# Choosing the experts' tokens in two halves: top-k on 48 partitions, a merge by a reversed list, and the first expert's rests on VectorE

## What is computed

```python
def _expert_choice(h, router_w, w1, w3, w2):
    ...
    C = max(1, EC_CAPACITY * N // N_EXPERTS)
    aff = jax.nn.softmax((xs @ router_w).astype(jnp.float32), axis=-1)
    gate, idx = lax.top_k(aff.T, C)
    xe = xs[idx]
    he = jax.nn.silu(jnp.einsum('ecd,edf->ecf', xe, w1)) * jnp.einsum('ecd,edf->ecf', xe, w3)
    ye = jnp.einsum('ecf,efd->ecd', he, w2) * gate[..., None].astype(h.dtype)
    out = jnp.zeros_like(xs).at[idx.reshape(-1)].add(ye.reshape(-1, D))
```

## Time and profile before

| | |
|---|---|
| median of 3 runs | 2005.06 us (2003.74 to 2011.64) |
| profiled execution: time, span | 2010.78 us, 2008.9 us |
| mean granted TensorE clock | 0.963 of 2.4 GHz |
| busy share TensorE, VectorE, ScalarE, GpSimd | 92%, 77%, 58%, 16% |
| mean DMA rate | 270 GB/s |

### The profile page before, as it was taken

One profiled execution on the slowest core, in us unless ns is written; L12 is line 12 of the kernel. 1 busy time (PEld: TensorE's weight loads), 2 busy tenths in 40 slices (PEclk: granted clock), 3 DMA queues, 4 the chain that ended last, 5 costly groups with the idle time before them and its releaser, 6 DMA issues.

```text
span 2008.9 us, 27163 instructions
## 1 busy us (share of the span) xinstructions
PE 1846.0 (92%) x9522; PEld 1304.3 (65%) x9522; DVE 1544.8 (77%) x2270; ACT 1156.3 (58%) x1540; POOL 326.2 (16%) x152
## 2 busy tenths in 40 slices
PE   4999999949999999999969999995999999999993
PEld 2776777836666666666657786784566666666662
DVE  4543646579999999999846364667899999999993
ACT  2410256337787877777642114623677777777772
POOL 0100021030212222121012003112122122122210
PEclk9999999969999999999989999996999999999997
DMA  9468201278999999999852721025799999999973
GB/s 342 163 226 321 84 1 31 107 289 332 368 385 379 376 378 383 386 386 377 289 188 87 261 80 79 9 108 231 296 378 370 386 374 386 376 388 380 383 299 128
DMA packets 86219, 542.02 MB, mean 270 GB/s; under 512 B 6880, under 2 KB 9698, under 8 KB 61572
## 3 DMA queue, kind: packets, MB, share of 16 engines
q1 hardware_dynamic: 75556, 504.10, 64.6%
q0 software_dynamic: 10592, 36.97, 6.8%
HBM read 517.19 MB, written 23.86 MB: 269 GB/s over the span
## 4 chain that ended last, share of the span: by engine, by line
PE 87%; DVE 7%; DMA 2%; ACT 2%; issue 1%; POOL 1%; SPq 0%; DVEq 0%; ACTq 0%
PE bank L1098 53%; PE bank L799 10%; PE bank L976 5%; PE bank L692 2%; PE bank L924 2%; PE bank L1115 1%; PE bank L835 1%; PE bank L939 1%; PE bank L909 1%; PE bank L1108 1%; PE bank L1014 1%; PE bank L997 1%; PE bank L1047 1%; DMA x_res<-arena_z,iscat 1%; DVE ring_r L1957 1%
## 5 line engine op out<-in xcount | busy, mean ns | idle before, releaser
L1378 ACT ACTIVATE arena_h_r<-ring 128x1024 fp32r<-128x1024 f32 x480 | 504.6, 1061 | 163.1 <-PE bank L1098 159.7
L1896 DVE TENSOR_TENSOR ring_r<-ring,arena_h_r 128x1024 fp32r<-128x1024 f32 x470 | 557.6, 1218 | 32.4 <-ACT arena_h_r L1378 25.3
L1098 PE MATMUL bank<-arena_h_r,arena_u_r 128*80 128x512 f32 x1280 | 372.8, 398 | 4.6 <-DVE arena_u_r L1916 4.6
L1896 DVE TENSOR_TENSOR ring_r<-ring,arena_u_r 128x1024 fp32r<-128x1024 f32 x282 | 333.8, 1219 | 13.7 <-ACT arena_u_r L1378 7.1
L1378 ACT ACTIVATE arena_u_r<-ring 128x1024 fp32r<-128x1024 f32 x288 | 301.2, 1059 | 61.0 <-PE bank L1098 61.0
L1098 PE MATMUL bank<-ring_r,arena_u_r 128*80 128x512 f32 x1024 | 318.4, 392 | 0.0
L1098 PEld LDWEIGHTS bank<-arena_h_r,arena_u_r 128*80 128x80 f32 x1280 | 188.2, 151 | 101.2 <-DVE arena_u_r L1916 6.2
L1098 PE MATMUL bank<-arena_u_r 128*80 128x512 f32 x768 | 216.9, 391 | 0.0
L1098 PEld LDWEIGHTS bank<-ring_r,arena_u_r 128*80 128x80 f32 x1024 | 151.9, 148 | 84.8 <-issue 0.7
L644 POOL DMA_INDIRECT x_res<-arena_z,iscat x32 | 91.6, 2861 | 643.3 <-DVE arena_z L1942 643.3
L1098 PE MATMUL bank<-arena_h_r,arena_z_r 128*80 128x512 f32 x640 | 181.2, 397 | 3.6 <-DVE arena_z_r L1931 3.6
(11 more groups left out here) (255 smaller groups left out, 2668.5 us busy)
## 6 DMA issues: line engine op xcount, KB each, us to landing
ring<-in_exp_w SPq DMA_DIRECT2D x192, 2048.0 KB, 10.1
ring<-in_ada_w SPq DMA_DIRECT2D x24, 2048.0 KB, 9.0
ring<-in_w_in SPq DMA_DIRECT2D x8, 2048.0 KB, 19.8
ring<-in_w_out SPq DMA_DIRECT2D x2, 4096.0 KB, 13.4
x_res<-arena_z POOLq DMA_DIRECT2D x10, 512.0 KB, 3.8
xn_dram<-arena_u POOLq DMA_DIRECT2D x10, 512.0 KB, 3.0
arena_z<-x_res SPq DMA_DIRECT2D x10, 512.0 KB, 6.1
arena_z<-x_res POOLq DMA_DIRECT2D x5, 512.0 KB, 3.6
```

Source lines behind the costliest of these rows:

```text
L1098: mm = pe.matmul(bank[out + n][0:CAP, :], xs[:, c, :], w[:, n * 512:(n + 1) * 512], start=(c == 0 and part == 0), stop=(c == KC - 1 and pa ...
L1378: act.activation(high[c], slot[s][:, c, :], ACT.Copy).then_inc(high_ready, 1)
L1896: v.tensor_tensor(slot_r[s][:, c, :], slot[s][:, c, :], high[c], ALU.subtract).then_inc(low_ready, 1)
```

## The change

The latents' affinities are transposed into two halves: latents 0 to 255 on partitions 0 to 15, latents 256 to 511 on partitions 32 to 47. One operation over 48 partitions and 256 columns then serves both, and each half yields its 64 best in descending order. The merge takes, for place i, the larger of the upper half's value i and the lower half's value 63 - i; that is exactly the set of the 64 best of both. For it the lists are turned to [64, 16] and the lower one is reversed by a matmul with a reversed unit matrix (`turn64`, a new 64x64 input loaded behind `w_out`). The context's list keeps its own two rounds, behind the merge, and its own trip through TensorE.

```diff
--- the top-k on VectorE
-                affinity_T(1, 0, LAT, bank[7][0:EXPERTS, :])
+                v.wait_ge(affT_mm, l * 2 + 1)
+                for at in (0, 32):
+                    ins = v.tensor_copy(affL[0][at:at + EXPERTS, :], bank[7][at:at + EXPERTS, 0:LHALF])
+                link(ins)
                 for turn in range(CAP_L // 8):
-                    top_round(turn, 0, LAT, 0, CAP_L)
+                    top_round(turn, affL, slice(0, TWO), 0, CAP_L)
...
-                    if turn == 4:
+                    if turn == 5:
                         h2(4)
-                    if turn == 5:
-                        logit_max(4, 5, bank[0][:, 0:EXPERTS])
-                    if turn == 6:
-                        affinity(2, 4, 5)
-                affinity_T(2, LAT, TOK, bank[5][0:EXPERTS, 0:P])
+                lists_cast()
+                logit_max(4, 5, bank[0][:, 0:EXPERTS])
+                lists_turned()
+                affinity(2, 4, 5)
+                lists_merged()
+                v.wait_ge(affT_mm, l * 2 + 2)
+                link(v.tensor_copy(affC[0], bank[5][0:EXPERTS, 0:P]))
--- the merge: upper = [64, 16] indices and values, turned_f and turned_v the reversed lower list
+                    v.tensor_tensor(first, g, turned_v, ALU.is_ge)
+                    v.tensor_tensor(gateT[0:CAP_L, :], g, turned_v, ALU.max)
+                    link(v.tensor_tensor(step, f, turned_f, ALU.subtract))
+                    link(v.tensor_tensor(step, step, first, ALU.mult))
+                    v.tensor_tensor(idxT[0:CAP_L, 0:EXPERTS], step, turned_f, ALU.add)
--- TensorE's order
                     w_out_half(n, 0)
+                    if n == 3:
+                        norm2_T(2)
+                        router(1)
                     w_out_half(n, 1)
...
-                w_out_half(4, 0)
+                router(2)
+                w_out_half(4, 0, 0, 6)
                 norm2_T(3)
-                router(2)
+                w_out_half(4, 0, 6, KC)
                 router(3)
-                w_out_half(4, 1, 0, KC // 2)
+                w_out_half(4, 1, 0, 3)
...
-                w_out_half(4, 1, KC // 2, KC)
+                w_out_half(4, 1, 3, KC)
+                pe.wait_ge(x1_done, l * NT + 4)
+                keep_clock(7, 1)
                 norm2_T(4)
-                pe.wait_ge(x1_done, l * NT + 4)
+                keep_clock(1, 1)
                 router(4)
--- the first matrix's rests on VectorE (GpSimd's first_rest and its calls are gone)
+                for c in range(4):
+                    first_rest(c)
                 rows(0, 0)
                 rows_rest(0, 0)
+                for c in range(4, KC):
+                    first_rest(c)
                 rest(w3_at(0), 1)
```

More of the change, by code:

```diff
@@ L188, in hybrid_prefix_diffusion_step @@
         g2e, s2e, xt = (sflat[:, a:a + KC * CAP].rearrange("p (c t) -> p c t", c=KC) for a in (640, 1280, 1920))
-        affT = [sflat[0:EXPERTS, a:a + TOK] for a in (0, 640)]
+        TWO = 32 + EXPERTS
+        LHALF = LAT // 2
+        affL = [sflat[0:TWO, a:a + LHALF] for a in (0, 256)]
+        affC = [sflat[0:EXPERTS, a:a + CTX] for a in (512, 1920)]
+        turn64 = sflat[0:CAP_L, 2048:2112]
+        upper, lower, picked = (sflat[0:CAP_L, a:a + 2 * EXPERTS] for a in (2112, 2144, 2176))
         gate1 = sb("gate1", [P, 2, D])
@@ L1064, in _ @@
                 router(3)
-                w_out_half(4, 1, 0, KC // 2)
+                w_out_half(4, 1, 0, 3)
                 pe.wait_ge(aff_done, l * 2 + 1)
                 for t in range(4):
-                    mm = pe.transpose(bank[7][0:EXPERTS, t * P:(t + 1) * P], aff[:, t, :], ident)
+                    at = t // 2 * 32
+                    mm = pe.matmul(bank[7][at:at + EXPERTS, (t % 2) * P:(t % 2 + 1) * P], aff[:, t, :], ident,
+                                   start=True, stop=True)
@@ L1074, in _ @@
+                for n, x in enumerate((topf, topv)):
+                    mm = pe.transpose(bank[1][0:CAP_L, n * EXPERTS:(n + 1) * EXPERTS], x[32:TWO, 0:CAP_L],
+                                      ident[32:TWO, 32:TWO])
+                mm.then_inc(top_mm, 1)
                 pe.wait_ge(aff_done, l * 2 + 2)
                 pe.transpose(bank[5][0:EXPERTS, 0:P], aff[:, 4, :], ident).then_inc(affT_mm, 1)
-                hold(pe, top_done, l + 1, const_in)
-                pe.transpose(bank[6][0:CAP, 0:EXPERTS], topf[:, :], ident[0:EXPERTS, 0:EXPERTS])
@@ L1079, in _ @@
-                pe.transpose(bank[6][0:CAP, EXPERTS:2 * EXPERTS], topv[:, :], ident[0:EXPERTS, 0:EXPERTS])\
-                    .then_inc(top_mm, 1)
+                pe.wait_ge(turn_in, l * 16 + 16)
+                pe.wait_ge(top_done, l * 3 + 2)
+                pe.matmul(bank[1][0:CAP_L, 2 * EXPERTS:4 * EXPERTS], turn64, lower, start=True, stop=True).then_inc(top_mm, 1)
+                pe.wait_ge(top_done, l * 3 + 3)
+                for n, x in enumerate((topf, topv)):
+                    mm = pe.matmul(bank[4][CAP_L:CAP, n * EXPERTS:(n + 1) * EXPERTS], x[0:EXPERTS, CAP_L:CAP],
+                                   ident[0:EXPERTS, 0:EXPERTS], start=True, stop=True)
@@ L1884, in _ @@
                 v.tensor_copy(icur[1][:, :], idxT[:, 1:2]).then_inc(icur_done, 1)
[L1885 to L1890, removed]
+                v.tensor_copy(gateT[CAP_L:CAP, :], bank[4][CAP_L:CAP, EXPERTS:2 * EXPERTS]).then_inc(top_out, 1)
                 def rest(m, s, after={}):
```

77 lines of the change are left out of this document (44 added, 33 removed).

## The result

The changed kernel took 2023.7 us (median of 6 runs, 2018.45 to 2026.03), the kernel before, run beside it, 2007.9 us (2003.74 to 2012.41). The ratio is 1.0085, 95% interval 1.0064 to 1.0105: slower by about 16 us, outside the forecast range of 1991 to 2016 us. The profiled execution took 2020.89 us with a span of 2019.1. One execution of a later kernel, e3, took 3130.72 us at a granted clock of 0.557 and stands outside its ratio.

A forecast was written before the change was run, and what follows sets the result against it. TensorE, busy 92% of the span, was taken as the bound, with VectorE 7% of the chain of waits. Per layer +7.4 - 9.7 + 3.3 - 1.0 = 0.0, so 2005 us, range 1991 to 2016 us.

The forecast's parts named there:

- What bounds the kernel: TensorE 87% of the chain, VectorE 7%, the latter between last output projection and first expert product, where the change works.
- Term 2: From the top-k's opening copy to the second icur column: 32.9 us becomes 23.2, -9.7 us per layer.
- Term 1: Up to the top-k's opening copy: it comes later through router 2's wait for h2(2) and a low clock, +7.4 us per layer.
- Term 3: From the second icur column to gathered rows: the gather is issued amid the weight reads, +3.3 us per layer.
- I: Time of the second icur column, which lets GpSimd gather; forecast to come 2.3 us earlier, at 436.1.
- T: Time of the copy that opens the top-k, 405.51 before; forecast 7.4 us later.
- Term 4: From gathered rows to the first expert product: rests in time, clock partly regained, -1.0 us per layer.
- F: Time of the first expert product, 448.55 before; forecast to stay within 3 us of 448.5.
- The clock stays low until the copy: Rival, before the top-k's opening copy: 12.3 us of work take 24.6, +8.0 us over the forecast's value, 2021 us; chance 0.08.
- The gather waits until the weight reads are through: Rival, at the gather: reads end at about 447, rows come 3 us later than forecast, 2011 us; chance 0.10.

The follow-up runs named there:

- e3: The changed kernel with the first expert's reads of w3 and w2 held until the first two gathers have landed; ratio 1.0153 against the kernel before.
- e11: The kernel before with the first expert's rests all on VectorE and nothing else changed; ratio 0.9993 against the kernel before.
- e8: e1 without the two new groups of filler matmuls; ratio 0.9971 against the kernel before.
- e1: The changed kernel with h2 of tile 2 moved ahead of tile 3's gated1 (VectorE) and norm2 (ScalarE); 1996.6 us, ratio 0.9951 against the kernel before.
- e2: The changed kernel with TensorE's old order of output projection, transposes and routers, all else kept; ratio 0.9971 against the kernel before.
- e4: The kernel before with only TensorE's new order of transposes, routers and output tiles 3 and 4; ratio 1.0115 against the kernel before.
- e10: e2 with chunks 5 to 7 of the first expert's w3 read early and w2's first half held; ratio 0.9938 against the kernel before.

## Why the prediction was wrong

Its forecast was no change, with -9.7 us of list work against +7.4 and +3.3 of new waits. Both waits were there; they were sized too small, and the range had not allowed for both at once.

- **What bounds the kernel: right.** All of the difference lies between the output projection and the first expert product, and layer 1 repeated layer 0 (+7.0 against +6.2). But only the list's 10 us were in the 33 us that VectorE's 7% pointed at; the 9.6 us came ahead of them and the 6.7 behind.
- **Term 2, the list, -9.7: right, -10.0.** MAX8 at 0.42 (0.41 forecast), independent of the number of partitions; casts at 0.18 (0.2); router 4's wait gone. The share given to the rests, 4.5 us, measured 4.7 in e11. The share given to the fillers, 1.8 us, measured 0.8 in e8.
- **Term 1, the start, +7.4: mechanism right, size off, +9.6.** The idle time was 7.35 us (7.5 forecast), router 2 lost 1.7 us (1.8), the chunks behind it ran low until 400.4 and lost 2.1 (2.5). What failed is the step "then 5 us of chunks low ... before it was back at 2.4": the clock came back at 400.8, and fell a second time behind router 3, where three more chunks took 3.7 us instead of 2.1 (407.19 to 410.88): 1.6 of the missing 2.2 us. The rest is small: a wait of 0.3 us for `h2(3)`, and 0.8 us instead of 0.4 for the affinity transposes. e1, e2 and e4 show that the whole term hangs on the place of one call, `h2(2)`. Why the clock fell again behind router 3 no run settles.
- **Term 3, the gather, +3.3: mechanism right, size off, +6.7.** What failed is "I take 8.3 us behind I", about half-way between the bounds 5.0 and 12; it was 11.9, of which 1.0 us passed before the issue (0.4 before) and 10.8 behind it. The nearest row was the loop's 11.6 us, a gather under reads, and not the 8.5 us write of a different size. At the gather's issue 5.0 MB of reads were still to come, on the flat end of the table above. And "all of it comes about 7 us later" failed too: against the first matmul of the output projection the write of tile 4's `xn` landed 11.0 us later, since T was 9.6 late and the write took 8.3 us instead of 3.9. The rule on queues in the Trainium skill (DMA: Bandwidth & Descriptors, Queues, rings and completion order), that an engine takes its queues in turn by packets, would have a gather of five rows per engine lose little beside the reads; no kernel here shows that, with 10.4 to 11.4 us under full reads against 4.3 to 4.8 without. The forecast was right to set it aside, and should have gone further.
- **Term 4, -1.0: -0.2 up to the product.** The rests were in time as forecast, and -0.6 + 0.4 is that -0.2. The other 0.8 us, for the clock behind F, did come back at first: the next row transposes started 14.2 and 14.5 us behind the first product (layers 0 and 1), where it was 15.4 in both. But at the end of the loop the clock stood at 1.2 GHz for 6.8 us instead of 3.4, and from the first product to the last only 0.3 us were left of it in layer 0 and nothing in layer 1.
- **The rivals.** Neither of the two that look like the outcome came as it was told. "The clock stays low until the copy" (2021 us, +8.0) did not: the clock came back, and the second fall cost 1.6 us. "The gather waits until the weight reads are through" (2011 us) has nearly the measured price, 3 us over my value against 3.4, but that is luck: it set the end of the reads at 447 and let the gather wait for it, while the last of those reads landed 7.7 us behind the rows' start. Each rival had a chance of its own and was priced alone; that both terms could be too small together was left out, and the range ended at 2016. With +2.2 in term 1, +3.4 in term 3 and the 0.8 of term 4 that lies behind F, less 0.3 in term 2, the forecast's sum of 0.0 becomes +6.1 per layer up to F, where the table above has +6.2. On 2007.9 us, what the kernel before took beside it, +6.2, +7.0 and 0.8 behind the last product make 2021.9; the median was 2023.7.
- **The point not seen at all:** that a shorter list by itself moves the gather into the reads and pays only in part (10 us off the list in e2, 7 back in the gather). The forecast had the reads end 7 us late because T was late; e2 shows the gather just as slow with T early.

## What to carry to other kernels

Before shortening a chain, write down what else starts from its beginning: here the weight reads and the top-k both hang on the end of the output projection, so 10 us off the one moved its gather into the other and 7 came back, and the old split of the rests fitted the old length as well. When a step is moved forward in one engine's order, look for its producer in the other engine's order and move that too; one `h2` call left behind cost 27 us of 2000 (1.0085 against 0.9951). And two risks in two links of one chain can come together; they add up and are not alternatives to be given a chance each.

## What the runs showed of the hardware

- A gather of 80 rows from GpSimd's queue takes 4.3 to 4.8 us from issue to the start of the row transposes with at most 0.3 MB of SyncE's reads left, and 10.4 to 11.4 with 2.7 to 5.6 MB left; it did not wait for these reads to end. The first packet on its queue starts 2.1 to 2.3 us behind the issue in the first case and 4.5 to 4.7 in the second.
- MAX8, MATCH_REPLACE8 and FIND_INDEX8 took 0.42, 0.40 and 0.41 us over 48x256 and 0.26 to 0.28 over 16x128; with 0.68 over 16x512 that goes by columns, and three times the partitions cost nothing.
- Two routers one behind the other do not fix the clock that follows. In e2's layer 0 they ran at the high clock throughout, where the kernel before took 4.51 us:

```profile
391.10 3.78 PE L1044 MATMUL bank<-rw,arena_h 128*128 128x16 f32 x32
```

  The same program took 69.4 us up to the first MAX8 in layer 0 and 71.0 in layer 1; e10 took 69.4 and 72.6, e11 72.3 and 70.7. The granted clock accounts for it: where it stayed at 2.4 GHz up to the opening copy (e2 and e10, layer 0) the stretch took 69.4 us, with 3.4 us at 1.2 GHz (e2 and e11, layer 1) 70.7 to 71.0, with 6.8 us (before, e11 layer 0, e10 layer 1) 72.3 to 72.6. A forecast for one such stretch has 3 us of play that no edit causes.
